# Denser turns of expert rows in the second pass of a decoder layer, with the first of them between the choices

## What is computed

```
def peer_ffn(x, w_query, sub_keys, expert_u, expert_v):
    q = (xt @ w_query).reshape(T, 8, 2, 128)
    s = einsum('thpd,hpnd->thpn', q, sub_keys)
    v_half, i_half = top_k(s, 16)               # per head and half
    cand = v_half[:, :, 0, :, None] + v_half[:, :, 1, None, :]
    top_s, top_pos = top_k(cand, 16)            # 8 heads x 16 = 128 experts a token
    gate = softmax(top_s)
    h = gelu(einsum('td,ted->te', xb, expert_u[eb]))
    y = einsum('te,ted->td', gb * h, expert_v[eb])
```

## Time and profile before

| | |
|---|---|
| median of 3 runs | 3145.13 us (3143.47 to 3148.01) |
| profiled execution | 3145.48 us |
| its span, first to last instruction | 3143.6 us |
| PE, DVE, ACT, POOL busy | 2694.7, 1272.7, 426.7, 803.9 us |
| moved by DMA | 1096.41 MB: 542.08 on the queue of weights, 551.94 on that of gathers |
| granted TensorE clock, mean | 0.929 of full speed |

### The profile page before, as it was taken

One profiled execution on the slowest core, in us unless ns is written; L12 is line 12 of the kernel. 1 busy time (PEld: TensorE's weight loads), 2 busy tenths in 40 slices (PEclk: granted clock), 3 DMA queues, 4 the chain that ended last, 5 costly groups with the idle time before them and its releaser, 6 DMA issues. The chain is left out here.

```text
span 3143.6 us, 37681 instructions
## 1 busy us (share of the span) xinstructions
PE 2694.7 (86%) x16328; PEld 2218.2 (71%) x16328; DVE 1272.7 (40%) x1693; ACT 426.7 (14%) x916; POOL 803.9 (26%) x536
## 2 busy tenths in 40 slices
PE   8899999998999999999898986788766767676566
PEld 7898899998889899889898885788422223222222
DVE  0122001010100155734443455447677775655654
ACT  1121100021000111111101210101100001211121
POOL 0000000000000011212211232233466565555652
PEclk9999999999999999999999988899888888888899
DMA  8976378776837799998998989999999999999996
GB/s 326 305 267 227 136 296 298 285 296 228 311 138 287 260 363 385 354 369 344 424 424 357 383 321 423 420 396 425 409 421 422 421 421 421 421 422 421 422 422 280
DMA packets 126932, 1096.41 MB, mean 349 GB/s; under 512 B 13440, under 2 KB 22064, under 8 KB 28080
## 3 DMA queue, kind: packets, MB, share of 16 engines
q1 hardware_dynamic: 50512, 542.08, 44.3%
q0 software_dynamic: 76256, 551.94, 42.9%
HBM read 1084.52 MB, written 9.44 MB: 348 GB/s over the span
## 5 line engine op out<-in xcount | busy, mean ns | idle before, releaser
L601 PE MATMUL PS<-arena 128*128 128x128 f32 (+1 forms) x13952 | 1883.7, 297 | 78.4 <-DMA arena<-units 64.5
L601 PEld LDWEIGHTS PS<-arena 128*128 128x128 f32 x13952 | 1798.6, 194 | 158.5 <-DMA arena<-units 57.7
L949 PE MATMUL PS<-arena 128*128 128x512 f32 x1152 | 628.6, 706 | 275.8 <-DMA arena<-peer_v,arena 264.2
L949 PEld LDWEIGHTS PS<-arena 128*128 128x128 f32 x1152 | 254.1, 228 | 649.3 <-issue 591.8
L1382 DVE CUSTOM_DVE_ANT_0 arena<-arena 128x2048 f32<-128x2048 f32 x256 | 586.8, 2292 | 287.5 <-DMA arena<-peer_u,arena 281.0
L566 POOL DMA_INDIRECT arena<-peer_u,arena x256 | 399.1, 1559 | 892.5 <-DVE arena L1382 678.2
L566 POOL DMA_INDIRECT arena<-peer_v,arena x256 | 393.8, 1538 | 449.3 <-PE PS L949 214.2
L1392 DVE SCALAR_TENSOR_TENSOR arena<-arena 128x2048 f32<-128x2048 f32 x112 | 263.4, 2352 | 132.0 <-DMA arena<-peer_v,arena 128.7
L972 ACT ACTIVATE arena<-PS 128x512 f32<-128x512 f32 (+2 forms) x154 | 84.5, 549 | 1313.5 <-PE PS L601 1199.9
L1347 ACT ACTIVATE arena<-arena 128x128 f32<-128x128 f32 x144 | 57.9, 402 | 722.9 <-PE PS L949 721.5
L537 POOL DMA_DIRECT2D arena<-ln_rows x2 | 1.3, 640 | 384.7 <-DVE arena L1727 384.7
(11 more groups left out here) (186 smaller groups left out, 1049.0 us busy)
## 6 DMA issues: line engine op xcount, KB each, us to landing
arena<-units SPq DMA_DIRECT2D x243, 2048.0 KB, 9.1
arena<-w_ukv SPq DMA_DIRECT2D x16, 512.0 KB, 10.4
arena<-ln_rows SPq DMA_DIRECT2D x6, 1024.0 KB, 14.8
arena<-ln_rows POOLq DMA_DIRECT2D x4, 1024.0 KB, 18.6
arena<-peer_u,arena POOLq DMA_INDIRECT x256, 23.5
arena<-peer_v,arena POOLq DMA_INDIRECT x256, 23.8
rb_scratch<-arena POOLq DMA_DIRECT2D x1, 3072.0 KB, 38.5
arena<-rb_scratch SPq DMA_DIRECT2D x12, 256.0 KB, 9.8
```

What stands on the lines that cost most here:

```text
L601: ins = mm(bank[:, first:first + rhs.shape[1]], lhs, rhs, start=k == 0, stop=k == KT - 1)
L949: ins = mm(Y[c], diag[:, n % 4 * P:(n % 4 + 1) * P], rows[b][:, c * 512:(c + 1) * 512], start=n == first_used[tb], stop=False, skip_group_ ...
```

## The change

- The turns in the second pass get denser up to the mixing projections, and go on from there to nothing: the three later groups of turns (in cross-attention, with its output projection and before the second norm's choice) find no row left, or are removed. Three turns of four rows stand between the choices of heads 1 to 3, ahead of the second pass.
- `gelu(0)` stands before the gates' evacuations in place of after them, since the 56th dot is earlier.
- `row_buffers()` counts the six halves of the weight ring as taken at `LATE`, so that the first late rows take the six slots.
- The last four rows of a block are shared between the engines as all others are, `LAST`, the identity products and `all_summed` are gone, and `last_norm` adds PSUM and the vector engine's sum, a quarter at a time, into the latter.
- Choices of the second block's heads 1 to 7 stand 6 dots apart in place of 8; `GATED` is 116 in place of 112.

```diff
--- before.py
+++ after.py
@@ -48,8 +48,7 @@
 HALF = 56
 FIRST = 72
 SOON = (NE - FIRST) // 2
-GATED = 112
-LAST = 4
+GATED = 116
 MASKED = -1e30
 TAKEN = -3e38
 
@@ -125,8 +124,6 @@
 
     if s < SOON:
         return True
-    if s % NE >= NE - LAST:
-        return False
     return s % 2 == 1 if s >= NE + 64 else s % 3 == 2
 
 
@@ -166,7 +163,7 @@
 
     count = SLOTS + 2 * RING
     held, loads, table = [None] * count, [0] * count, {}
-    taken = [-1] * count
+    taken = [-1] * SLOTS + [LATE] * (2 * RING)
     for n, row in enumerate(ARRIVALS):
         b = min(range(SLOTS if n < LATE else count), key=lambda i: taken[i])
         table[row] = (b, loads[b], held[b])
@@ -392,7 +389,7 @@
         chosen, tops_rd, gexp_done, weighed = (sem(n) for n in ("chosen", "tops_rd", "gexp_done", "weighed"))
         row_landed = [sem(f"row_landed{n}") for n in range(SLOTS + 2 * RING)]
         dot_done, gelu_done, v_summed, v_used = (sem(n) for n in ("dot_done", "gelu_done", "v_summed", "v_used"))
-        gated, all_summed = sem("gated"), sem("all_summed")
+        gated = sem("gated")
         gh_done, diag_done = sem("gh_done"), sem("diag_done")
         var3_done, root3_done, fin_done = sem("var3_done"), sem("root3_done"), sem("fin_done")
 
@@ -949,12 +946,6 @@
                         ins = mm(Y[c], diag[:, n % 4 * P:(n % 4 + 1) * P], rows[b][:, c * 512:(c + 1) * 512],
                                  start=n == first_used[tb], stop=False, skip_group_check=True)
                     ins.then_inc(v_used, 1)
-                if e == NE - LAST:
-
-                    pe.wait_ge(v_summed, summed_to(s))
-                    for c in range(4):
-                        ins = mm(Y[c], ident, sums[tb][:, c * 512:(c + 1) * 512], start=False, stop=False, skip_group_check=True)
-                    ins.then_inc(all_summed, 1)
 
 
         @block.scalar
@@ -1250,6 +1241,7 @@
                     squares(q)
                     index_queries(1, 3)
                     mean_roots(q)
+                    gelu(0)
 
                 for j in range(4):
                     for n in range(2):
@@ -1268,8 +1260,6 @@
                         if s < 4 * (tb + 1):
                             relu_out(tb, s)
 
-                if tb:
-                    gelu(0)
                 q_out(tb, 0)
                 gate_out(tb, 0)
                 for j in range(1, 4):
@@ -1533,13 +1523,13 @@
                     link(v.tensor_scalar(a_f[:, cols], a_sf[:, cols], omlb[:, h:h + 1], lb[:, h:h + 1], ALU.mult, ALU.add))
                 mark(v.tensor_scalar(a_k, a_f, -1.0, 1.0, ALU.mult, ALU.add), f_ready, q + 1)
                 if tb:
-                    turn(2)
+                    turn(3)
                 if old:
                     masked_scores(q)
                     next_states(q)
                     gated_sums(q)
                 if tb:
-                    turn(2)
+                    turn(3)
                 if tb and j < 2:
                     choose(0, 4 + 2 * j)
                 dve.wait_ge(gate_rd, q + 1)
@@ -1688,19 +1678,19 @@
                 masked_scores(q)
                 next_states(q)
                 if tb:
-                    turn(4)
+                    turn(3)
                 gated_sums(q)
                 if tb:
-                    turn(4)
+                    turn(3)
                 normed_out(q)
                 if tb:
-                    turn(4)
+                    turn(3)
 
                 for s in range(8):
                     if s < 4 * (tb + 1):
                         accumulate_scores(tb, s)
                     if s == 0 and tb:
-                        turn(2)
+                        turn(3)
                     if s % 2:
                         j = s // 2
                         dve.wait_ge(evac_done, evacuated(tb, "WA", j))
@@ -1718,7 +1708,7 @@
                     if g + 1 < groups:
                         next_biases(tb, g + 1)
                     if tb:
-                        turn(3)
+                        turn(4)
 
                 for j in range(4):
                     dve.wait_ge(evac_done, evacuated(tb, "WB", j))
@@ -1755,13 +1743,16 @@
             trunk(0)
             for k in range(1, 4):
                 choose(0, k)
+                turn(4)
             trunk(1)
             turn(LATE)
             gate(1)
 
-            def last_norm(tb, parts, done):
-
+            def last_norm(tb, banks, done):
+
+                parts = [sums[tb][:, c * 512:(c + 1) * 512] for c in range(4)]
                 for c in range(4):
+                    link(v.tensor_tensor(parts[c], parts[c], banks[c], ALU.add))
                     link(v.bn_stats(stats[:, 48 + 6 * c:54 + 6 * c], parts[c]))
                 mark(v.bn_aggr(mv3, stats[:, 48:72]), var3_done, tb + 1)
                 dve.wait_ge(fin_in, 32)
@@ -1778,18 +1769,17 @@
             for kind, s in ARRIVALS[LATE:]:
                 if kind == "U":
                     dot(s)
-                    if s % 8 == 1 and s // 8 - NE // 8 < PEER_HEADS - 1:
-                        choose(1, s // 8 - NE // 8 + 1)
+                    k, more = divmod(s - NE, 6)
+                    if more == 1 and k < PEER_HEADS - 1:
+                        choose(1, k + 1)
                 else:
                     if s == GATED + 8:
                         weigh(1)
                     if s == NE + PK:
-                        dve.wait_ge(all_summed, 1)
                         dve.wait_ge(v_used, used_to(NE - 1))
                         last_norm(0, B, acc)
                     if on_vector(s):
                         add_row(s)
-            dve.wait_ge(all_summed, 2)
             dve.wait_ge(v_used, used_to(TB * NE - 1))
             last_norm(1, PJ, fin_x)
 # ---- launch: one core ----
```

## The result

The changed kernel takes 3179.09 us (median of 4 runs, 3173.66 to 3179.79) against 3145.74 us of the kernel before (4 runs, 3143.47 to 3148.01): a ratio of 1.0102, with a 95% interval of 1.0085 to 1.0120. It is 1% slower. The profiled execution took 3179.79 us, its span is 3178.0 us, 34.4 more than before. All times are medians of the fast executions; one execution each of b4_behind and b3_slots_only that took over 10 ms is left out.

The account below looks back on a forecast made before the run. The end was taken as bound by bytes (421 to 422 GB/s), earlier stretches as having some DMA room. Span 3143.6 + 64 - 15 - 7.4 - 4.8 = 3180.4, adjusted to a median of 3182 us; range 3146 to 3208.

Parts of the forecast that it names:

- Between the choices, +36: Start of the second pass: late-landing rows delay norms to 1205 and the first block's last product to 1277, +36 us.
- The rival by which rows get half of the bytes: Beside weights a row lands each 4.97 us, row 12 at 1176; S falls by 22, time 3160; chance 0.12.
- Three further blocks, +12: Later recurrence blocks: one more dot between gate and scan, two blocks also end a choice later; +4 us each.
- Scores, +13: Score stage without DMA room: five to six of nine more rows must land before the selection is done, +13 us.
- Groups, +8: Eight attention groups: a fourth row hides in 9.0 us of idle time once landed; +8 us (nothing, to 35).
- Branch and mixing projections, -3: Same turns in the same order, with some three rows fewer in flight: -3 us.
- S: Shift of the first part's end, the point at 1990.5 us where mixing is added up: 64 us, bounds 17 and 110.
- Second part, -15: Cross-attention and queries without rows: waits for loads go, -15 us (-10 to -18).
- Late rows, -7.4: After the trunk: first gather issued 7.7 us later, 350 instead of 356 rows at 2.51 us each (-15.1); net -7.4 us.
- the end, -4.8: After the last row lands: a vector-engine sum and four adds precede the statistics, which end 4.8 us sooner.
- the room was not filled: Answers a rival: empty DMA room before the end of mixing is filled, S toward 17, 3135; S 17 to 35 chance 0.16.
- the groups did not go bad: Answers a rival: four rows at 7.4 us overrun each attention group, costing 35 us, not 8; about 3210 and more; chance 0.12.

Follow-up runs that it names:

- b4_behind: Kernel before, with the third turn of each recurrence block moved behind the products (2, 2, 4 in place of 2, 2, 2, 2): 3134.74 us.
- b3_slots_only: Kernel before, with only the row slots first for the late rows: 3142.5 us, ratio 0.9994, interval includes 1.
- a2_behind: Changed kernel, with the third turn of each recurrence block moved behind the products (3, 3, 6 in place of 3, 3, 3, 3): 3171.37 us.
- a4: Changed kernel, with turns of 2 in place of 3 in the score stage alone: 3155.65 us.
- c1: Kernel before, with turns of 3 in place of 2 in the score stage alone (27 rows in place of 18): 3168.46 us.
- c2_groups_only: Kernel before, with turns of 4 in place of 3 in the eight attention groups alone: 3146.27 us, not told apart from before.
- b2_end_only: Kernel before, with the change of the end alone (last four rows shared, no identity products, PSUM added by the vector engine): 3140.67 us.
- a1: Changed kernel without the three turns of four rows between the choices; the 12 rows move to cross-attention: 3151.27 us.
- b1: Kernel before, with the three turns of four rows between the choices alone: 3164.68 us.
- b5_all: Kernel before, with third turn behind the products, slots first for late rows, and the new end together: 3127.69 us.
- c3_more_early: b5_all with turns of 4 in the attention groups and 32 early sums in place of 28 (160 early rows): 3109.42 us.

## Why the prediction was right

The forecast was 3182, measured 3179.09. Step by step, against the trace of the changed kernel:

- **Between the choices, +36.** The dots end as reckoned. Here are the last two of them, the norms, and the products, in the vector engine's timeline:

```profile
1195.71 2.29 DVE L1372 CUSTOM_DVE_ANT_0 arena<-arena 128x2048 f32<-128x2048 f32 x1 [5.07 <-DMA arena<-peer_u,arena]
...
1203.10 2.29 DVE L1372 CUSTOM_DVE_ANT_0 arena<-arena 128x2048 f32<-128x2048 f32 x1 [5.09 <-DMA arena<-peer_u,arena]
...
1205.43 0.29 DVE L1462 BATCH_NORM_STATS2 arena<-arena 128x6 f32<-128x128 f32 x1
```
```profile
1274.27 2.87 DVE L1553 TENSOR_TENSOR arena<-arena 128x512 f32<-128x512 f32 x4 [4.07 <-ACT arena L1056]
```

  This is 1203.10 for the twelfth dot (1203), 1205.43 for the norms (1205), and a first product that ends at 1277.14 (1277), 36.6 us late. The rows land 7.4 us apart, as in the earlier trace rows. The rival by which rows get half of the bytes, the plain reading of the Trainium skill's page "DMA: Bandwidth & Descriptors" ("Queues, rings and completion order"), had 1176 for the twelfth row; the trace does not agree with it.
- **Three further blocks, +12:** the fourth product is 50.7 us late, +14.1. a2_behind shows that the third turn is the cause of it: without that turn ahead of the products the three blocks take 211.2 us in place of 224.7, and 210.6 before. It takes 7.6 us off the first step too.
- **Scores, +13:** too small. In the changed kernel the stage took 18.6 us more, and the nine rows are worth 18.4 us there by a4 and 27.1 by c1. The step counted five to six rows where nearly all nine have to be taken before the selection (their bytes are 22 us), as the stage has no room.
- **Groups, +8:** too large. From the selection to the first branch sum it took 4.9 us less than before, 197.7 against 202.6, and c2_groups_only shows that a fourth row is free there. The 9.0 us of idle time before each group's sum, which I had read rightly, cover it.
- **Branch and mixing projections, -3:** +2.6 (from the first branch sum, 1850.7 and 1915.1, to the end of mixing). S is 67.0, forecast 64. That it came out so close is in part luck: the groups were 12.9 us too large, while the blocks, the scores and the projections were 2.1, 5.6 and 5.6 too small, and these errors cancel. The rounding of the sum of 66 down to 64 had no reason given.
- **Second part, -15:** -17.5, at 263 GB/s; both waits for loads are gone.
- **Late rows, -7.4, and the end, -4.8:** together -15.1 against -12.2. The queue starts again 8.6 us after the trunk, as the timeline there shows beside the earlier trace rows:

```profile
2269.80 1.28 ACT L970 ACT_TABLE_LOAD   x1
...
2272.29 18.24 PE L946 MATMUL PS<-arena 128*128 128x512 f32 x38 [2.98 <-issue]
...
2277.93 0.93 POOL L563 DMA_INDIRECT arena<-peer_v,arena  x1 [228.21 <-PE PS L946]
...
2286.95 2.35 DVE L1382 SCALAR_TENSOR_TENSOR arena<-arena 128x2048 f32<-128x2048 f32 x1 [10.48 <-DMA arena<-peer_v,arena]
```

  Before, V28 had been issued 0.9 us ahead of the trunk's end, so the delay is 9.5 where I had 7.7. At the end, beside the earlier trace rows, the last row's sum begins at 3160.10 and the statistics end at 3168.24, 8.1 us later; b2_end_only has the same 8.15:

```profile
3160.10 2.35 DVE L1382 SCALAR_TENSOR_TENSOR arena<-arena 128x2048 f32<-128x2048 f32 x1 [2.58 <-DMA arena<-peer_v,arena]
3162.48 0.69 DVE L1755 TENSOR_TENSOR arena<-arena,PS 128x512 f32<-128x512 f32 x1
...
3167.55 0.69 DVE L1756 BATCH_NORM_STATS2 arena<-arena 128x6 f32<-128x512 f32 x1
```

  The restart was later than forecast, but the first gather after the pause took 0.93 us to issue in place of 2.75, and V35 is summed at 2286.95, 17.6 us after the trunk's end; from there to the last row it is 2.51 us a row ((3160.10 - 2286.95) / 348), as taken. The delay in the stream of rows was so about 5 us and not 7.7.

The other rivals: the room was not filled, as S below 27 would have asked (401 GB/s in 943 us leave 49 us empty; 47 were forecast), and the groups did not go bad (197.7 us in place of 202.6). By a1 and b1 the bytes alone do not decide. By c1 and a4 a row more in the score stage costs about what its bytes take, or somewhat more.

What stays open: how much of the 27 us of c1_scores_only is bytes and how much the standing of SyncE's queue was not separated, as no run moved the wait for the selection behind the weights. That ScalarE's wait for the last choice costs b4_behind its 6.5 us was read from the timeline, not tried. The earlier `gelu(0)` and the choices 6 dots apart are in every a run and were never tried alone. For the choices the late rows speak, which came at the rate forecast; for `gelu(0)` no run tells.

## What to carry to other kernels

Free bytes in a stage are worth something only where the engine that takes the rows has idle time ahead of a step that another engine waits for: here a fourth row in an attention group is free, while one between a gate and its products costs much of its length (moving 12 rows of 2.37 us behind the products gave back 21.1 us at the fourth block, moving 8 gave 12.0), and one in a stage whose DMA is full costs at least about its bytes. Move rows first out of the chain and into idle places, then ask whether more can be early; the same 156 early rows made this kernel 1% slower or, in b5_all, which also has the new end and the slots first, 0.6% faster. With 160 early rows and the denser groups (c3_more_early) it is 1.2% faster; then 346 gathers are left after the trunk, against 356 before.

## What had not been expected of the hardware

Rows that run beside weight loads land 7.3 us apart in the mean from the third dot between the choices (1137.48) to the twelfth (1203.10), and 7.4 us apart in the score stage, while 425 and 424 GB/s are moved in all. The prediction had carried this pace from the one stage to the other, and it held. A row of 1.049 MB in 7.4 us is a third of those bytes; two thirds are left for the weights. With the weights gone a row takes 2.51 us.
